# DeltaNet recurrence: both slots of filler of a chunk behind the new values' product, and the state's product with the queries behind the signal to VectorE

## The chip, the cores and the metric

The kernel runs on one core of one Trainium2 chip. A core has TensorE (matrix products, written PE in the profile, its weight loads PEld), VectorE (DVE), ScalarE (ACT), GpSimd (POOL) and SyncE (SP), which here issues most of the DMAs. Each engine works through a queue of its own in order; semaphores tie them together. The metric is the device time of one execution in microseconds (us), lower is better.

## The reference, cut to what matters

One layer of a hybrid decoder on 1024 positions of width 1024. Its second branch is a gated delta rule with four heads of dimension 128:

```
def step(state, inp):
    u_i, w_i, qd_i, qk_i, kt_i, gl_i = inp
    v_new = u_i - jnp.einsum('bhcd,bhde->bhce', w_i, state)
    o = jnp.einsum('bhcd,bhde->bhce', qd_i, state) + jnp.einsum('bhcj,bhje->bhce', qk_i, v_new)
    state = state * jnp.exp(gl_i)[..., None, None] + jnp.einsum('bhcd,bhce->bhde', kt_i, v_new)
    return state, o
```

It is a scan over chunks: each chunk's new values need the state, and the next state needs the new values. Around it stand a gMLP branch, stick-breaking attention, a wide input projection, a gated mix and a feed-forward network with 4096 hidden channels, all of them large products.

## The kernel before

The large products are made from blocks of 128 output channels. Each float32 operand is split into an upper and a lower part, so that one block is 2 halves of the positions x 8 slices of the depth = 16 steps, and one step is three 128x512 matmuls (`product_step`, lines 351 to 353). ScalarE makes the upper part of a block's weights (line 325), VectorE the lower (line 329), ScalarE evacuates each finished half (line 397, after steps 7 and 15 of the block).

In the phase that this change touches, the input projection's blocks of pairs 14 to 25 (384 steps) are executed beside the DeltaNet heads, as filler. Every engine walks the same list `DN_SLOTS` of weights: each call of `beside()` takes the next weight and executes as many steps as the rounded running sum allows. A weight of 1.2 is thus one step, now and then two. TensorE issues the matmuls of the steps, ScalarE and VectorE what belongs to them.

The heads i = 0 to 3 follow one another. A head first prepares its factors for all its chunks (two groups g of four chunks each, stages in `DN_STAGES`: Gram matrices, the triangular inverse by levels, the factor w), then scans its 8 chunks of 128 positions (n = 0 to 7). In the scan, chunk n on TensorE is:

- from chunk 1 on, a wait for the state (`dn_scan_ev`), then the state's product with the queries into the output bank (line 1369),
- the product of `d_TT` with `d_vb` (line 1370) and, from chunk 1 on, that of `d_wt` with the state (line 1372), which together are the new values; then a signal to VectorE,
- `beside()`, the first slot,
- a wait for VectorE's copy of the new values into `d_vn` (line 1782),
- the new values' share of the output (line 1376) and the state's product (line 1378), then a signal; VectorE makes the state `d_S` from it (line 1786 in chunk 0, line 1789 later),
- behind chunks 2 and 4 of heads 0 to 2 two sums of squares for the next head, and behind chunk 6 of each head one for the output's norm (line 1317),
- `beside()`, the second slot.

After chunk 7 follow a last slot of weight 4 and one more sum of squares. ScalarE uses the scan to activate the next head's inputs (lines 950 and 953), to load the function table and activate `d_z` (line 1008) and to make inverse roots (lines 959 and 962). VectorE has a piece of the next head's work behind each state (1699, 1703 and 1704, 1709, 1720, 1724), and both slots of a chunk behind that.

Of the kernel before, what the change touches and what calls it, by code (L numbers as in the profile page):

```python
# [13 lines left out]
NCH = S // P  # L14
# [44 lines left out]
def hybrid_decoder_layer(nc, xT, w_stream, w_bd, w_spT, cols_in, consts_in, outT):  # L59
# [12 lines left out]
    def sb(name, shape, dt=f32):  # L72
        return scope[0].enter_context(nc.sbuf_tensor(name, shape, dt))
# [4 lines left out]
    with top:  # L78
# [48 lines left out]
        with scope[0]:  # L127
            d_x = [sb(f"d_x{s}", [P, S]) for s in range(2)]
            d_z = sb("d_z", [P, S])
            d_q = sb("d_q", [P, S])  # L130
# [15 lines left out]
            d_S = sb("d_S", [P, P])  # L146
# [339 lines left out]
        def pe_beside(pe, b):  # L486
            for step in b.steps():
                blk, r = divmod(step, 16)
                hf, k = divmod(r, 8)
                n, s = b.n0 + blk // 2, blk % 2  # L490
                if k == 0:
                    pe.wait_ge(bank_read[hf], 1 + 2 * n + s)
                product_step(pe, n, s, hf, k, act_hi, act_lo)
# [50 lines left out]
        NDS = len(DN_STAGES)  # L544
# [3 lines left out]
        DN_FUNCS = (ACT.Identity, ACT.Gelu, ACT.Identity) * 4  # L548

        DN_PRO = [12, 3, 8]  # L550
        DN_HEAD = [2, 3, 1, 2, 1, 2, 1, 5] + [0, 2.72] * (NDS - 5) + [0, 1.5] + [1.2] * (2 * NCH) + [4]
        DN_SLOTS = DN_PRO + DN_HEAD * 4

        def dn_use(i, x):

            return 2 + DN_USES * i + x + 1

        def o_use(i):

            return dn_use(i, NDS + 2 if i < 3 else NDS)  # L560
# [606 lines left out]
        def _(pe):  # L1167
# [10 lines left out]
            for hf in range(2):  # L1178
                pe.wait_ge(bank_read[hf], 1)
                t = slice(HALF * hf, HALF * hf + HALF)  # L1180
                for k in range(KT):
                    for s in range(2):
# [7 lines left out]
                        o = first_banks[s][hf][:]  # L1190
# [33 lines left out]
            for n in range(NCH):  # L1224
                for part in range(2):
                    last = nc.tensor.matmul(c_bank[:, 8 * n:8 * n + 8], bdT[:, P * n:P * n + P], ident[0:16, 8 * part:8 * part + 8],
                                            start=(part == 0), stop=(part == 1))
# [80 lines left out]
            def beside():  # L1308
                pe_beside(pe, b)

            def chunk(t, n):
                return t[:, P * n:P * n + P]

            def squares_sum(g, sq, use):

                pe.wait_ge(dn_taken[g], use)
                nc.tensor.matmul(d_bank[g][:], ones[:], sq[:, HALF * g:HALF * g + HALF], start=True, stop=True).then_inc(dn_prod[g], 1)
# [8 lines left out]
            for i in range(4):  # L1326
                for x, name in enumerate(DN_STAGES):
                    for g in range(2):
                        pe.wait_ge(dn_taken[g], dn_use(i, x))
                        if name == "gram":  # L1330
                            pe.wait_ge(dn_ks, i + 1)
                        if name == "qk":
                            pe.wait_ge(dn_qs, i + 1)
                        if name == "vT":
                            pe.wait_ge(dn_silu, 3 * i + 3)
                        if name == "t0":
                            pe.wait_ge(dn_tt[g], i + 1)
                        if name[0] == "x":
                            pe.wait_ge(dn_b[g], (N_LEV - 1) * i + int(name[1:]))
                        for m in range(4):  # L1340
                            n = 4 * g + m
                            o = d_bank[g][:, P * m:P * m + P]
                            if name == "gram":
                                last = nc.tensor.matmul(o, chunk(d_x[1], n), chunk(d_x[1], n), start=True, stop=True)
                            elif name == "qk":
                                last = nc.tensor.matmul(o, chunk(d_x[1], n), chunk(d_q, n), start=True, stop=True)
                            elif name == "kT":
                                last = nc.tensor.transpose(o, chunk(d_x[1], n), ident)
                            elif name == "vT":
                                last = nc.tensor.transpose(o, chunk(d_x[2], n), ident)  # L1350
                            elif name[0] == "t":
                                last = nc.tensor.transpose(o, d_TT[:, n, :], ident)  # L1352
                            elif name[0] == "x":
                                last = nc.tensor.matmul(o, d_B[:, n, :], d_T[:, n, :], start=True, stop=True)  # L1354
                            elif name[0] == "y":
                                last = nc.tensor.matmul(o, d_X[:, n, :], d_TT[:, n, :], start=True, stop=True)  # L1356
                            else:
                                last = nc.tensor.matmul(o, d_kb[:, n, :], d_TT[:, n, :], start=True, stop=True)
                        last.then_inc(dn_prod[g], 1)
                        beside()  # L1360
                for n in range(NCH):
                    o = (z_bank[1] if n < 4 else c_bank)[:, P * (n % 4):P * (n % 4) + P]
                    if n == 1:
                        pe.wait_ge(dn_q, 2 * i + 2)
                        for g in range(2):
                            pe.wait_ge(dn_taken[g], 1 + dn_use(i, NDS - 1))
                    if n:
                        pe.wait_ge(dn_scan_ev, 15 * i + 2 * n)
                        nc.tensor.matmul(o, d_S[:], chunk(d_q, n), start=True, stop=False)
                    last = nc.tensor.matmul(z_bank[0][:, 0:P], d_TT[:, n, :], d_vb[:, n, :], start=True, stop=(n == 0))  # L1370
                    if n:
                        last = nc.tensor.matmul(z_bank[0][:, 0:P], d_wt[:, n, :], d_S[:], start=False, stop=True)
                    last.then_inc(dn_scan_mm, 1)
                    beside()
                    pe.wait_ge(dn_scan_ev, 15 * i + 2 * n + 1)
                    last = nc.tensor.matmul(o, d_vn[:], d_qk[:, n, :], start=(n == 0), stop=True)
                    if n < NCH - 1:
                        last = nc.tensor.matmul(z_bank[0][:, P:2 * P], d_kt[:, n, :], d_vn[:], start=True, stop=True)
                    last.then_inc(dn_scan_mm, 1)
                    if n in (2, 4) and i < 3:  # L1380
                        j = n // 2 - 1
                        pe.wait_ge(dn_sq, 2 * i + 2 + j + 1)
                        for g in range(2):
                            squares_sum(g, d_r[j], dn_use(i, NDS + j))
                    if n == 6:
                        pe.wait_ge(dn_osq, 2 * i + 1)
                        squares_sum(0, d_kb[:].rearrange("p n c -> p (n c)"), o_use(i))
                    beside()
                beside()
                pe.wait_ge(dn_osq, 2 * i + 2)  # L1390
                squares_sum(1, d_kb[:].rearrange("p n c -> p (n c)"), o_use(i))
# [17 lines left out]
            for b in range(4):  # L1409
# [3 lines left out]
                for hf in range(2):  # L1413
                    for m in range(4):
                        n = 4 * hf + m
# [14 lines left out]
            for i in range(2):  # L1430
                for q in range(6):
                    n, s = PAIR_BR + 3 * i + q // 2, q % 2
# [713 lines left out]
```

## Time and profile before

| | us |
|---|---|
| median of 3 runs | 1964.14 |
| lowest and highest | 1963.74, 1964.51 |
| the profiled execution | 1964.16 |
| its span in the profile | 1962.4 |

The span is the time between the first and the last instruction in the profile; the 1.8 us around it are start and end of the program. The four scans lie at about 559 to 588, 671 to 701, 782 to 811 and 891 to 917 us of the span. In the profile a product of 128x128 float32 shows as two matmuls (x2), a row names the first one's start, and a matmul's end is modelled, so distances between starts are to be read, not durations.

### The profile page before, as it was taken

The page shows a single profiled execution, that of the slowest core. Times are in us where ns is not written, and L with a number is a line of the kernel's source. Part 1 is how long each engine was busy: PE and PEld are TensorE (multiplying, and loading weights), DVE is VectorE, ACT ScalarE, POOL GpSimd, SP SyncE. Part 2 cuts the span into 40 slices and gives each one's busy share as a digit, 9 for nine tenths or more (in the row PEclk, how much of TensorE's full clock was granted, in tenths as well). Part 3 has the DMA queues.
Part 4 walks back from the last instruction along what each step waited for, and adds up shares of the span by engine and source line. Part 5 has one row for each costly group of instructions (what it writes and reads, how often), then busy time and mean ns, then how long its engine had stood idle before and what let it go on. Part 6 is the DMA issues. An engine that isn't in the chain of part 4 may idle for free.

```text
span 1962.4 us, 25291 instructions
## 1 busy us (share of the span) xinstructions
PE 1936.0 (99%) x9862; PEld 1576.8 (80%) x9862; DVE 945.3 (48%) x1267; ACT 759.5 (39%) x1165; POOL 83.2 (4%) x63
## 2 busy tenths in 40 slices
PE   9999999999999999999999999999999999999996
PEld 7887777777888888888787888888888888888885
DVE  6715566575445354523546654774333223223347
ACT  6325555554353543533334334543232113102322
POOL 0000000001203121120000000000000000000000
PEclk9999999999999999999999999999999999999998
DMA  5223122213122221223434444432311111111144
GB/s 193 98 97 118 51 92 97 103 49 140 65 97 86 97 87 65 86 74 129 153 133 152 134 147 149 150 130 92 107 45 52 53 43 46 50 53 43 49 155 150
DMA packets 62352, 191.75 MB, mean 98 GB/s; under 512 B 6768, under 2 KB 6832, under 8 KB 62256
## 3 DMA queue, kind: packets, MB, share of 16 engines
q1 hardware_dynamic: 59952, 186.23, 27.3%
q10 hardware_dynamic: 2304, 4.20, 0.6%
q8 instruction: 65, 1.06, 0.2%
q14 instruction: 31, 0.25, 0.0%
HBM read 146.33 MB, written 44.07 MB: 97 GB/s over the span
## 4 chain that ended last, share of the span: by engine, by line
PE 94%; DVE 3%; ACT 1%; issue 1%; DMA 1%; DVEq 0%; ACTq 0%; SPq 0%
PE gemm L351 18%; PE gemm L353 18%; PE gemm L352 18%; PE gemm L595 6%; PE gemm L597 5%; PE gemm L596 5%; PE dn L1354 2%; PE dn L1356 2%; PE z L1253 2%; PE gemm L1442 2%; PE dn L1275 2%; PE gemm L1443 2%; PE gemm L1444 2%; PE dn L1352 1%; PE attn_out L1287 1%; PE cumsum L1287 1%
## 5 line engine op out<-in xcount | busy, mean ns | idle before, releaser
L351 PE MATMUL gemm<-act_hi,w_hi 128*128 128x512 f32 x1216 | 500.9, 412 | 0.5 <-issue 0.5
L353 PE MATMUL gemm<-act_hi,w_lo 128*128 128x512 f32 x1216 | 476.1, 392 | 0.0
L352 PE MATMUL gemm<-act_lo,w_hi 128*128 128x512 f32 x1216 | 474.8, 390 | 0.0
L329 DVE TENSOR_TENSOR w_lo<-w_raw,w_hi 128x1024 fp32r<-128x1024 f32 x174 | 217.3, 1249 | 194.0 <-ACT w_hi L325 190.5
L325 ACT ACTIVATE w_hi<-w_raw 128x1024 fp32r<-128x1024 f32 x174 | 183.1, 1052 | 280.8 <-PE gemm L353 153.2
L353 PEld LDWEIGHTS gemm<-act_hi,w_lo 128*128 128x128 f32 x1216 | 228.6, 188 | 49.6
L351 PEld LDWEIGHTS gemm<-act_hi,w_hi 128*128 128x128 f32 x1216 | 229.5, 189 | 45.8 <-issue 6.7
L352 PEld LDWEIGHTS gemm<-act_lo,w_hi 128*128 128x128 f32 x1216 | 229.7, 189 | 43.0 <-issue 3.3
L397 ACT ACTIVATE stage<-gemm,cols 128x512 f32<-128x512 f32 x104 | 71.6, 688 | 239.7 <-PE gemm L353 235.6
L1117 ACT ACTIVATE f_t<-f_t 128x512 f32<-128x512 f32 x64 | 40.4, 632 | 218.0 <-DVE f_t L1959 218.0
L1629 DVE TENSOR_TENSOR_SCAN a_P<-a_keep,a_P,a_floor 128x512 f32<-128x512 f32 (+3 forms) x96 | 94.0, 1008 | 37.6 <-ACT a_keep L912 37.2
L595 PE MATMUL gemm<-act_hi,w_hi 128*128 128x512 f32 x256 | 101.3, 396 | 0.9 <-DVE w_lo L329 0.7
L2065 POOL TENSOR_TENSOR d_bB<-d_at,consts 128x512 f32<-128x512 f32 x48 | 66.5, 1404 | 793.3 <-DVE d_at L1761 630.5
L595 PE MATMUL gemm<-f_hi,w_hi 128*128 128x512 f32 x256 | 100.0, 391 | 0.0
L597 PE MATMUL gemm<-act_hi,w_lo 128*128 128x512 f32 x256 | 99.7, 390 | 0.0
L596 PE MATMUL gemm<-act_lo,w_hi 128*128 128x512 f32 x256 | 99.7, 389 | 0.0
L597 PE MATMUL gemm<-f_hi,w_lo 128*128 128x512 f32 x256 | 99.6, 389 | 0.0
L596 PE MATMUL gemm<-f_lo,w_hi 128*128 128x512 f32 x256 | 99.6, 389 | 0.0
L351 PE MATMUL gemm<-f_hi,w_hi 128*128 128x512 f32 x256 | 99.6, 389 | 0.0
L352 PE MATMUL gemm<-f_lo,w_hi 128*128 128x512 f32 x256 | 99.6, 389 | 0.0
L353 PE MATMUL gemm<-f_hi,w_lo 128*128 128x512 f32 x256 | 99.6, 389 | 0.0
L1775 DVE TENSOR_TENSOR d_TT<-d_TT,dn 128x512 f32<-128x512 f32 x48 | 33.0, 688 | 134.7 <-PE dn L1356 134.7
(280 smaller groups left out, 2888.1 us busy)
## 6 DMA issues: line engine op xcount, KB each, us to landing
w_raw<-w_stream SPq DMA_DIRECT2D x174, 512.0 KB, 3.4
projections<-stage SPq DMA_DIRECT2D x60, 512.0 KB, 2.9
gate<-projections SPq DMA_DIRECT2D x48, 256.0 KB, 2.7
d_in<-projections SPq DMA_DIRECT2D x12, 512.0 KB, 6.8
x_fin<-xT SPq DMA_DIRECT2D x8, 512.0 KB, 4.3
residual<-mixed ACTq DMA_DIRECT2D x16, 256.0 KB, 2.0
act_hi<-residual SPq DMA_DIRECT2D x8, 512.0 KB, 4.9
outT<-mixed SPq DMA_DIRECT2D x16, 256.0 KB, 2.0
```

The source lines that it names most:

```text
L325: nc.scalar.activation(w_hi[s][:], w_raw[s][:].rearrange("p (k c) -> p k c", k=KT), ACT.Copy).then_inc(hi_ready[s], 1)
L329: nc.vector.tensor_tensor(w_lo[s][:], w_raw[s][:].rearrange("p (k c) -> p k c", k=KT), w_hi[s][:].bitcast(f32), ALU.subtract).then_inc(lo_ ...
L351: nc.tensor.matmul(g_bank[hf][:], w_hi[s][:, k, :], a_hi[:, k, t], start=(k == 0), stop=False)
L352: nc.tensor.matmul(g_bank[hf][:], w_hi[s][:, k, :], a_lo[:, k, t], start=False, stop=False)
L353: last = nc.tensor.matmul(g_bank[hf][:], w_lo[s][:, k, :], a_hi[:, k, t], start=False, stop=(k == KT - 1))
L397: nc.scalar.activation(stage[s][:, HALF * hf:HALF * hf + HALF], g_bank[hf][:], func, bias=cols[:, ds(V_BIN + 2 * (n + shift) + s, 1)]).the ...
L595: nc.tensor.matmul(g_bank[s][:], w_hi[s][:, k, :], a_hi[:, k, t], start=(k == 0), stop=False)
L596: nc.tensor.matmul(g_bank[s][:], w_hi[s][:, k, :], a_lo[:, k, t], start=False, stop=False)
L597: last = nc.tensor.matmul(g_bank[s][:], w_lo[s][:, k, :], a_hi[:, k, t], start=False, stop=(k == KT - 1))
L1117: nc.scalar.activation(f_t[slot][:], f_t[slot][:], ACT.Square).then_inc(f_sqr, 1)
L1629: nc.vector.tensor_tensor_scan(run[:, off:off + n][:, ::-1], a_keep[Y % 4][:, 0:n][:, ::-1], floor[:, ::-1], run[:, off + n:off + n + 1], ...
L2065: nc.gpsimd.tensor_tensor(d_B[:, c, :], d_at[:, c, :], consts[:, None, C_LEV + lev, :].broadcast_to([P, 4, P]), ALU.mult).then_inc(dn_b[g], 1)
```

## The change

In the scan the two slots of a chunk had a weight of 1.2 each. Now the first has 2.4 and the second 0.0; the sum is the same, so that all steps outside the scan stay in their slots. And the state's product with the queries no longer stands ahead of the new values' products, but behind their signal and ahead of the first slot. The wait for the state stays where it was, ahead of the chunk's first product.

```diff
-        DN_HEAD = [2, 3, 1, 2, 1, 2, 1, 5] + [0, 2.72] * (NDS - 5) + [0, 1.5] + [1.2] * (2 * NCH) + [4]
+        DN_HEAD = [2, 3, 1, 2, 1, 2, 1, 5] + [0, 2.72] * (NDS - 5) + [0, 1.5] + [2.4, 0.0] * NCH + [4]
...
                     if n:
                         pe.wait_ge(dn_scan_ev, 15 * i + 2 * n)
-                        nc.tensor.matmul(o, d_S[:], chunk(d_q, n), start=True, stop=False)
                     last = nc.tensor.matmul(z_bank[0][:, 0:P], d_TT[:, n, :], d_vb[:, n, :], start=True, stop=(n == 0))
                     if n:
                         last = nc.tensor.matmul(z_bank[0][:, 0:P], d_wt[:, n, :], d_S[:], start=False, stop=True)
                     last.then_inc(dn_scan_mm, 1)
+                    if n:
+                        nc.tensor.matmul(o, d_S[:], chunk(d_q, n), start=True, stop=False)
                     beside()
```

The orders below give the lines of each kernel's own code: behind the moved product, 1370, 1372, 1369, 1376 and 1378 of before are 1369, 1371, 1374, 1377 and 1379 of after. TensorE, head 0, from chunk 1's share of the output to chunk 2's first slot, before:

```order
L1376 MATMUL z<-d_qk,d_vn 128x128 [waits dn_scan_ev]
L1378 MATMUL z<-d_vn,d_kt 128x128
L351 MATMUL gemm<-act_hi,w_hi 128x512
L352 MATMUL gemm<-act_lo,w_hi 128x512
L353 MATMUL gemm<-act_hi,w_lo 128x512
L1369 MATMUL z<-d_q,d_S 128x128 [waits dn_scan_ev]
L1370 MATMUL z<-d_vb,d_TT 128x128
L1372 MATMUL z<-d_S,d_wt 128x128
L351 MATMUL gemm<-act_hi,w_hi 128x512
L352 MATMUL gemm<-act_lo,w_hi 128x512
L353 MATMUL gemm<-act_hi,w_lo 128x512
```

The same place after:

```order
L1377 MATMUL z<-d_qk,d_vn 128x128 [waits dn_scan_ev]
L1379 MATMUL z<-d_vn,d_kt 128x128
L1369 MATMUL z<-d_vb,d_TT 128x128 [waits dn_scan_ev]
L1371 MATMUL z<-d_S,d_wt 128x128
L1374 MATMUL z<-d_q,d_S 128x128
L351 MATMUL gemm<-act_hi,w_hi 128x512
L352 MATMUL gemm<-act_lo,w_hi 128x512
L353 MATMUL gemm<-act_hi,w_lo 128x512
L351 MATMUL gemm<-act_hi,w_hi 128x512
L352 MATMUL gemm<-act_lo,w_hi 128x512
L353 MATMUL gemm<-act_hi,w_lo 128x512
```

The step (351 to 353) between the state's product on `d_kt` and the wait for `dn_scan_ev` is gone from there and has become one more step in the first slot; the product of `d_q` with `d_S` now follows the other two.

ScalarE, head 2, around its chunk 0, before (`stage` is the evacuation of a finished half, `w_hi` the upper part of the next weights, `d_z`, `d_x` and `d_r` belong to the head itself):

```order
L1008 ACT_TABLE_LOAD
L1008 ACTIVATE d_z<-d_z 128x1024 [waits dn_z]
L950 ACTIVATE d_x<-d_x 128x1024 [waits dn_conv]
L953 ACTIVATE d_r<-d_x 128x1024 [waits dn_silu]
L397 ACTIVATE stage<-gemm,cols 128x512 [waits blk_done0]
L325 ACTIVATE w_hi<-w_raw 128x1024 [waits blk_done0,raw_loaded0]
L950 ACTIVATE d_x<-d_x 128x1024 [waits dn_conv]
```

After:

```order
L397 ACTIVATE stage<-gemm,cols 128x512 [waits blk_done0]
L325 ACTIVATE w_hi<-w_raw 128x1024 [waits blk_done0,raw_loaded0]
L1008 ACT_TABLE_LOAD
L1008 ACTIVATE d_z<-d_z 128x1024 [waits dn_z]
L950 ACTIVATE d_x<-d_x 128x1024 [waits dn_conv]
L953 ACTIVATE d_r<-d_x 128x1024 [waits dn_silu]
L950 ACTIVATE d_x<-d_x 128x1024 [waits dn_conv]
```

The evacuation and the weight split of the step that moved to the first slot now stand ahead of the table load and of the head's own activations. There are six such moves on ScalarE in the four scans; VectorE's and SyncE's orders are the same in both kernels.

## Rows read from the trace of the kernel before

**Rows 1.** The page's head: the span, then busy time of each engine.
```profile
span 1962.4 us, 25291 instructions
...
PE 1936.0 (99%) x9862; PEld 1576.8 (80%) x9862; DVE 945.3 (48%) x1267; ACT 759.5 (39%) x1165; POOL 83.2 (4%) x63
```

**Rows 2.** Waits of TensorE's weight loads, 550 to 930: us, times, longest.
```profile
PEld z L1376 <- DVE d_vn L1782: 1.8, 3, 1.3
```

**Rows 3.** Timeline, head 3, chunks 4 to 6: start us, duration us, engine, line.
```profile
902.43 0.39 PE L1372 MATMUL z<-d_S,d_wt 128*128 128x128 f32 x2
...
903.58 0.39 PE L1378 MATMUL z<-d_vn,d_kt 128*128 128x128 f32 x2
...
904.00 0.35 DVE L1789 SCALAR_TENSOR_TENSOR d_S<-d_S,d_last,z 128x128 f32<-128x128 f32 x1 [0.85 <-PE z L1378]
...
904.40 0.30 PEld L1369 LDWEIGHTS cumsum<-d_q,d_S 128*128 128x128 f32 x2 [0.18 <-DVE d_S L1789]
904.50 0.40 PE L1369 MATMUL cumsum<-d_q,d_S 128*128 128x128 f32 x2
...
904.96 0.39 PE L1372 MATMUL z<-d_S,d_wt 128*128 128x128 f32 x2
...
906.77 0.39 PE L1378 MATMUL z<-d_vn,d_kt 128*128 128x128 f32 x2
```

**Rows 4.** Timeline, head 1, chunk 1: VectorE's queue held by a DMA.
```profile
673.34 0.39 PE L1372 MATMUL z<-d_S,d_wt 128*128 128x128 f32 x2
...
673.72 1.23 DVE L1699 TENSOR_TENSOR d_dt<-d_gB,bd_gc 128x1024 f32<-128x1024 f32 x1 [1.05 <-DMA d_bB<-decay_beta_rows]
...
675.65 0.39 PE L1378 MATMUL z<-d_vn,d_kt 128*128 128x128 f32 x2
```

**Rows 5.** Timeline, head 0: the copy behind chunk 0, then chunk 1's products.
```profile
560.54 0.29 DVE L1786 COPY d_S<-z 128x128 f32<-128x128 f32 x1 [0.86 <-PE z L1378]
...
561.50 0.39 PE L1372 MATMUL z<-d_S,d_wt 128*128 128x128 f32 x2
...
562.78 0.39 PE L1378 MATMUL z<-d_vn,d_kt 128*128 128x128 f32 x2
```

**Rows 6.** Timeline of TensorE: sums of squares behind chunks 2 and 6.
```profile
566.23 1.88 PE L1317 MATMUL dn<-d_r,ones 128*128 128x512 f32 x4
...
568.64 0.38 PE L1369 MATMUL z<-d_q,d_S 128*128 128x128 f32 x2
...
909.51 1.02 PE L1317 MATMUL dn<-d_kb,ones 128*128 128x512 f32 x2
...
911.07 0.38 PE L1369 MATMUL cumsum<-d_q,d_S 128*128 128x128 f32 x2
```

**Rows 7.** Timeline of VectorE, head 1, behind chunk 6.
```profile
693.44 0.35 DVE L1789 SCALAR_TENSOR_TENSOR d_S<-d_S,d_last,z 128x128 f32<-128x128 f32 x1 [0.83 <-PE z L1378]
693.71 1.22 DVE L1720 TENSOR_TENSOR d_dt<-d_dt,consts 128x1024 f32<-128x1024 f32 x1
694.96 1.23 DVE L329 TENSOR_TENSOR w_lo<-w_raw,w_hi 128x1024 fp32r<-128x1024 f32 x1
```

**Rows 8.** Timeline, head 2, chunk 0: TensorE's first product, then ScalarE.
```profile
781.76 0.38 PE L1370 MATMUL z<-d_vb,d_TT 128*128 128x128 f32 x2
...
781.87 1.28 ACT L1008 ACT_TABLE_LOAD   x1
...
786.17 0.67 ACT L397 ACTIVATE stage<-gemm,cols 128x512 f32<-128x512 f32 x1
...
787.69 1.05 ACT L950 ACTIVATE d_x<-d_x 128x1024 f32<-128x1024 f32 x1
```

**Rows 9.** Timeline, start of head 1: a weight load behind a bank's wait.
```profile
589.55 0.97 PEld L1344 LDWEIGHTS dn<-d_x 128*128 128x128 f32 x8 [1.67 <-ACT d_wt L959]
```

**Rows 10.** Stretches: engines' busy us, granted clock (the number after POOL), DMA.
```profile
130.80:137.60 6.80, 6.80 (x24) 5.90 (x25) 1.53 (x4) 4.53 (x7) 0.00 (x0) 0.50 0.97 360
...
671.00:696.00 25.00, 24.10 (x132) 18.73 (x132) 9.64 (x20) 17.99 (x22) 0.00 (x0) 1.00 0.45 162
```

## The prediction, made before the changed kernel had run

> **What bounds the kernel now.** I read four views in this order. The page's head gives the size of the question: TensorE is busy 1936.0 of 1962.4 us, so whatever makes it stand still in the recurrence is added to the end, and what makes another engine faster is not taken off it [rows 1]. The waits of TensorE's weight loads over the whole stretch of the four heads tell how much there is to gain: its longest entry from the chunks is 1.8 us in 3 waits for the new values [rows 2]. So both hand-overs to VectorE in a chunk are covered today, each by one step of filler (three 128x512 matmuls). The timeline of one chunk shows by how much, and that is the row set on which the forecast rests [rows 3]. The timelines of chunks with a wait, of the chunks that have other products between state and next chunk, and of ScalarE's queue give the exceptions [rows 4 to 8]. I call the heads 0 to 3 and the chunks 0 to 7, "new values" the copy on line 1782, "state" the update on line 1789 (a copy on 1786 in chunk 0).
>
> **Units, from [rows 3].** Two 128x128 products lie between 904.50 and 904.96, so one takes 0.23 us. From a chunk's last product before the filler to its state product is 1.15 us with one step (902.43 to 903.58) and 1.81 us with two (904.96 to 906.77): a step costs 0.67 us when it joins another. The state product starts at 903.58 and has left TensorE at 903.80; VectorE starts the state at 904.00 and needs 0.35; the load of the product that waits for it stands at 904.40 and the product at 904.50. From 903.80 to 904.50 are 0.70 us, and the one filler step there covers them (0.67 us and 0.03 of hand-over).
>
> **Part 1, the filler step behind the state product goes away.** The change leaves the wait for the state in front of the chunk's first product (the order shows it there, now on the product of d_TT with d_vb, though this one reads no state). The distance of 0.70 us is made of VectorE's answer and the load, neither of which the filler shortened, so TensorE stands still for it. It applies where nothing else lies between: not behind chunks 2 and 4 of heads 0 to 2, where two sums of squares take 568.64 - 566.23 - 0.67 = 1.74 us, and not behind chunk 6 of any head, where one takes 911.07 - 909.51 - 0.67 = 0.89 us [rows 6]; both are longer than 0.70. Seven boundaries by four heads are 28; less 6 and less 4 leave 18. Four of them follow chunk 0, whose copy takes 0.29 instead of 0.35 us [rows 5]: 0.64 each. 14 x 0.70 + 4 x 0.64 = **+12.4 us**. Bounds: if the answer came as fast as a product's own end allows in [rows 3] less the 0.10 between load and product, 0.60 each, +10.6; if each wait cost 0.10 more, +14.2.
>
> **Part 2, the same step stands behind the new values' product.** The steps are the same 19 or 20 a head and each is still executed; in its new place it costs 0.67 us instead of 0.70, since it shares the hand-over: 28 x 0.03 = **-0.8 us** (between 0 and -0.8).
>
> **Part 3, the new values get more cover.** In a chunk with one step in that place, TensorE now has 0.67 us more filler and 0.23 us of the state's product with the queries, which moves behind the signal. Moving it costs nothing by itself, it is one product either way. It removes the waits that exist. In head 1 the row differences wait for a DMA and hold VectorE's queue (line 1699 at 673.72), so that chunk 1 takes 675.65 - 673.34 = 2.31 us instead of 1.15: 1.16 us [rows 4]. The DMA's time doesn't move, TensorE comes 1.3 us later by then (one step and one wait) and has two further steps: all of it goes. In head 0 the same place has 562.78 - 561.50 = 1.28, 0.13 too much [rows 5]. Together **-1.3 us** (0 to -2).
>
> **Part 4, one place where cover gets thinner.** Everything that VectorE does between the state and the next new values (up to 1.2 us for a split, scaling or mask) used to hide under two steps and three products; now it hides under one chunk's first slot. With two steps there TensorE needs the new values 0.15 + 3 x 0.23 + 1.37 = 2.2 us after the state's end (904.35 in [rows 3]); with one 1.25 us instruction between, VectorE has them ready for a product after 1.25 + 0.29 + 0.15 = 1.7. It holds. In head 1 behind chunk 6 there are two (the mask at 693.71, the weight split at 694.96) [rows 7]. VectorE would finish the new values 0.47 + 1.25 + 1.23 + 0.29 = 3.24 us after the square sum starts, the dependent product comes 0.15 later: 3.39. TensorE is there after 0.89 + 3 x 0.23 + 2 x 0.67 + 0.03 = 2.95. **+0.45 us** (0 to 1). VectorE's and SyncE's own orders don't change; no load or store is issued in another place.
>
> **Part 5, ScalarE.** Six evacuations move ahead of the head's own activations. The hardest is head 2, chunk 0: the evacuation and the weight split now stand ahead of the table load. The head's first product starts at 781.76. Today ScalarE runs on at once, from the table load at 781.87 to the end of the square at 786.17, and then 1.5 us of evacuation and split until 787.69 [rows 8]. Then it would wait for the head's second step, which ends at 781.76 + 0.23 + 0.03 + 1.34 = 783.4, be done with both at 785.1, and with the square 4.3 us later, at 789.4. TensorE needs that square behind chunk 2. Chunk 0 takes it 0.23 + 2.04 + 0.46 (three steps), the wait 0.64; chunks 1 and 2 take 0.69 + 1.37 + 0.46 each (two steps), the wait between them 0.70: 781.76 + 9.11 = 790.9. **0**, with 1.5 us to spare; if that cover were gone, up to 1.6 us, the time ScalarE now stands in front of the step, and the same once more in head 1.
>
> **Sum.** 12.4 - 0.8 - 1.3 + 0.45 = +10.8 us. Against the profiled execution, 1964.16 us with a span of 1962.4, it gives 1975.0; that execution is within 0.1 us of the median of 1964.14, so the sum holds for both.
>
> **A rule weighed.** In every case of this trace where TensorE waits on a semaphore, the weight load waits too: the load of line 1344 needs only keys that have long been there, the wait is for a PSUM bank, and the load still stands idle 1.67 us until ScalarE has emptied it [rows 9]. The Trainium skill, "TensorE: Matmul & The Clock Gate", section "Architectural detail: the array is 16x 32x32, not 1x 128x128", states that TensorE's queue is a partial reorder window and can pull weight loads ahead of matmuls in flight. By that rule the load of d_TT, which needs no state, would slip in front of the wait. The trace's row speaks against it here.
>
> **Rivals.**
> (a) The load goes ahead of the wait. The distance from load to product in [rows 3], 904.40 to 904.50, is saved 18 times, 1.8 us: 1973.2. Against it: [rows 9].
> (b) ScalarE falls behind by the bounds of part 5, 2 x 1.6 us: 1978.2. For it: it waits for filler before the activations that the sums of squares need. Against: TensorE itself is slower by then, and there is 1.5 us to spare.
> (c) The clock falls. In head 1's chunks the granted clock is 1.00, that is 2.4 GHz; one stretch of 6.80 us in the trace has 0.50, that is 1.2 GHz [rows 10]. Such a stretch costs half its length, 3.4 us; one in each head gives 1975.0 + 13.6 = 1988.6. For it: TensorE stands still for a fifth of a chunk. Against: the wait of 1.16 us in head 1 lies in that stretch and left the clock at 1.00.
> (d) Not slower. The state's wait is cheaper than I read: TensorE still has matmuls in flight when the wait begins, and if the answer cost nothing beyond them, the parts 2 to 4 would be left, -1.65 us: 1962.5. It decides at a price of 1.65 / 18 = 0.09 us a boundary. Against: VectorE starts 0.20 us after the product has left and needs 0.35, two terms that nothing on TensorE can hide.
> That the change doesn't do what it says is excluded by the order: the filler rows between the two products are gone.
>
> **How the numbers follow.** Forecast 0.74, (a) 0.08, (b) 0.12, (c) 0.03, (d) 0.03. The forecast's own bounds: the 0.60 to 0.80 of part 1 is -1.8 to +1.8, the parts 2 to 4 add -0.9 to +1.9, not all at once; I take 1972.2 to 1978.4, which holds (a) and most of (b) and leaves out (c), (d) and the ends. A measurement of this kernel tells 0.2% (3.9 us) from no change; only (d) lies within it. Slower 0.96, same 0.03, faster 0.01.
>
> **What would show it.** In the profile after, TensorE's weight load of the product of d_TT with d_vb waits for the state in about 18 places, 0.5 to 0.7 us each, about 11 us in all; the waits for new values shrink to one in head 1, chunk 7; the chunk with two steps takes 3.2 us instead of 2.5; the square sums have no wait on ScalarE in front; the granted clock stays 1.00. It would be wrong if these waits were short, or if the heads' stretches grew by something other than them.

## The result, and the profile after

| | before | after |
|---|---|---|
| median | 1963.89 us (5 runs, 1962.45 to 1964.51) | 1973.81 us (5 runs, 1973.40 to 1975.41) |
| profiled execution, span | 1962.4 us | 1971.6 us |

The changed kernel takes 1.0053 times as long (95% interval 1.0039 to 1.0068): 9.9 us more, where 10.8 were forecast. The head of the page after, to be held against [rows 1]: the engines' busy times differ by 3.2 us at most (TensorE's matmuls 1938.6 against 1936.0), the span is 9.2 us longer.

```profile
span 1971.6 us, 25291 instructions
...
PE 1938.6 (98%) x9862; PEld 1580.0 (80%) x9862; DVE 944.3 (48%) x1267; ACT 759.4 (39%) x1165; POOL 83.1 (4%) x63
```

The waits of TensorE's matmuls over the four heads (engine, what waited, for whom: us in total, times, longest). Both entries are new; a matmul's end is modelled, so they show the number of the stills better than their length:

```profile
PE z L1369 <- DVE d_S L1790: 6.2, 14, 0.4
PE z L1369 <- DVE d_S L1787: 1.9, 4, 0.5
```

The product of `d_TT` with `d_vb` waits 14 times for the state's update and 4 times, behind chunk 0, for its copy: 18 stills. The same view of the weight loads, as in [rows 2], needs care:

```profile
PEld z L1369 <- DVE d_S L1790: 10.5, 18, 0.6
PEld z L1369 <- issue: 5.4, 16, 0.6
...
PEld cumsum L1377 <- DVE d_vn L1783: 0.5, 1, 0.5
```

Its 18 waits for the state are not the 18 stills. They are 14 of 0.63 us and 4 of 0.41 behind chunk 6, where the sum of squares still runs and no matmul waits; the four stills behind chunk 0, of 0.64 us each on the load, stand under "issue". The waits for new values of [rows 2] are down to one of 0.5 us.

One chunk and the next in head 3, to be held against [rows 3] (start us, duration us, engine, line):

```profile
905.58 0.38 PE L1377 MATMUL z<-d_qk,d_vn 128*128 128x128 f32 x2
...
905.80 0.39 PE L1379 MATMUL z<-d_vn,d_kt 128*128 128x128 f32 x2
...
906.23 0.35 DVE L1790 SCALAR_TENSOR_TENSOR d_S<-d_S,d_last,z 128x128 f32<-128x128 f32 x1 [2.44 <-PE z L1379]
...
906.63 0.30 PEld L1369 LDWEIGHTS z<-d_vb,d_TT 128*128 128x128 f32 x2 [0.63 <-DVE d_S L1790]
...
906.95 0.39 PE L1371 MATMUL z<-d_S,d_wt 128*128 128x128 f32 x2
...
908.79 0.38 PE L1377 MATMUL z<-d_qk,d_vn 128*128 128x128 f32 x2
```

The order is now 1377, 1379, then nothing, then 1369 and 1371. From the state product's start to the start of the product of `d_wt` with the state are 906.95 - 905.80 = 1.15 us; two products, the state's and 1369, take 0.45 of it, so 0.70 us stand still. VectorE's answer is what it was: it starts 0.43 after the product's start (0.42 in [rows 3]) and the load starts 0.05 after its end. The load does not read the state and waits all the same.

How long the scans take is read from TensorE's timeline, from the start of a head's first product of `d_TT` with `d_vb` to that of its last sum of squares. For head 3, before:

```profile
891.00 0.38 PE L1370 MATMUL z<-d_vb,d_TT 128*128 128x128 f32 x2
...
916.80 1.02 PE L1317 MATMUL dn<-d_kb,ones 128*128 128x512 f32 x2
```

and after, 29.96 instead of 25.80 us:

```profile
896.17 0.38 PE L1369 MATMUL z<-d_vb,d_TT 128*128 128x128 f32 x2
...
926.13 1.02 PE L1317 MATMUL dn<-d_kb,ones 128*128 128x512 f32 x2
```

| head | 0 | 1 | 2 | 3 | sum |
|---|---|---|---|---|---|
| before, us | 28.72 | 29.68 | 28.54 | 25.80 | 112.74 |
| after, us | 31.28 | 31.65 | 31.25 | 29.96 | 124.14 |
| difference | 2.56 | 1.97 | 2.71 | 4.16 | 11.40 |

The scans alone lose 11.4 us. The rest of the span is 1849.7 us before and 1847.5 after, 2.2 less, in code that the change doesn't touch; what the profiles show of it is in the last section.

### The profile page after: what moved, and what is told of

It reads as the page before. It is cut to its first block, busy times and chain, and to the rows that moved or that the text cites. A ratio compares the mean times of both kernels' runs of the same rounds, so it can differ in the third digit from the quotient of the medians.

```text
span 1971.6 us, 25291 instructions
## 1 busy us (share of the span) xinstructions
PE 1938.6 (98%) x9862; PEld 1580.0 (80%) x9862; DVE 944.3 (48%) x1267; ACT 759.4 (39%) x1165; POOL 83.1 (4%) x63
## 4 chain that ended last, share of the span: by engine, by line
PE 94%; DVE 3%; ACT 1%; issue 1%; DMA 0%; DVEq 0%; ACTq 0%; SPq 0%
PE gemm L351 18%; PE gemm L353 18%; PE gemm L352 18%; PE gemm L595 6%; PE gemm L596 5%; PE gemm L597 5%; PE dn L1354 2%; PE dn L1356 2%; PE z L1253 2%; PE gemm L1443 2%; PE dn L1275 2%; PE gemm L1445 2%; PE gemm L1444 2%; PE dn L1352 1%; PE attn_out L1287 1%; PE cumsum L1287 1%
```

## The experiments

All of them are read twice: by the median against runs of the kernel before on the same chip, and by the sum of the four scans in the profiled execution. The second is the sharper one: the same TensorE and VectorE order gave 124.14 and 124.15 us in two kernels (after and e4). The groups of experiments ran on different chips, and a difference of medians between two of them, say e6 less after, is rougher than one to the kernel before.

| kernel | slots | sum of scans, us | less before | median, us | ratio, 95% interval |
|---|---|---|---|---|---|
| before | 1.2, 1.2 | 112.74 | | 1963.3 to 1963.9 | |
| after | 2.4, 0.0 | 124.14 | +11.40 | 1973.81 | 1.0053 (1.0039 to 1.0068) |
| e1, slots alone | 2.4, 0.0 | 124.19 | +11.45 | 1973.21 | 1.0052 (1.0035 to 1.0069) |
| e2, product alone | 1.2, 1.2 | 113.07 | +0.33 | 1962.47 | 0.9996 (0.9986 to 1.0006) |
| e3, slots mirrored | 0.0, 2.4 | 126.34 | +13.60 | 1976.84 | 1.0070 (1.0054 to 1.0087) |
| e4, ScalarE's old order | 2.4, 0.0 | 124.15 | +11.41 | 1974.62 | 1.0061 (1.0044 to 1.0078) |
| e5, head 3 alone | mixed | 116.96 | +4.22 | 1966.97 | 1.0019 (1.0010 to 1.0028) |
| e6, free product ahead | 2.4, 0.0 | 120.24 | +7.50 | 1970.00 | 1.0035 (1.0021 to 1.0048) |
| e7, and state product first | 2.4, 0.0 | 116.01 | +3.27 | 1965.80 | 1.0015 (1.0005 to 1.0024) |
| e8, both reorderings | 1.2, 1.2 | 112.87 | +0.13 | 1962.65 | 0.9997 (0.9988 to 1.0006) |
| e9, and rows later | 1.2, 1.2 | 111.25 | -1.49 | 1961.09 | 0.9987 (0.9978 to 0.9996) |
| e10, and tiny products mixed | 1.2, 1.2 | 111.20 | -1.54 | 1960.48 | 0.9989 (0.9980 to 0.9998) |
| e11, mixed finer | 1.2, 1.2 | 111.19 | -1.55 | 1962.26 | 0.9994 (0.9985 to 1.0003) |

**Each half of the change alone.** The slots without the moved product:

```diff
-        ... + [0, 1.5] + [1.2] * (2 * NCH) + [4]
+        ... + [0, 1.5] + [2.4, 0.0] * NCH + [4]
```

> One part alone: the slots are 2.4 and 0.0 as in the changed kernel, the state's product with the queries stays ahead of the new values' products. Theory (TensorE stands still 0.70 us for the state at 18 boundaries, since the filler behind the state product is gone): +12.4 for the stills, -0.8 for shared hand-overs, -1.3 for the waits for new values that go, +0.7 in head 1 chunk 7, where the product no longer gives 0.23 us of cover: +11.0 us on before, and 18 waits for the state of about 0.6 us each on the weight loads. Rival (the moved product is what costs): no more than +1 us.

Measured: +11.45 us in the scans, the same as the whole change. The waits of TensorE's matmuls, where the product with the queries (1369 here, as in the kernel before) meets the state's wait:

```profile
PE cumsum L1369 <- DVE d_S L1789: 4.0, 9, 0.4
PE z L1369 <- DVE d_S L1789: 2.2, 5, 0.4
PE z L1369 <- DVE d_S L1786: 1.9, 4, 0.5
```

Nine, five and four are the 18 places. The slots are the whole loss, and the moved product has no part in it.

The moved product alone is the changed kernel with `[1.2] * (2 * NCH)` put back.

> The other part alone: the state's product with the queries moves behind the signal, the slots stay 1.2 and 1.2. Theory: it costs nothing by itself and gives each wait for new values 0.23 us of cover; the wait in head 1 chunk 1 falls from 1.16 to 0.93 us, the 0.13 in head 0 goes: -0.4 us on before, not to be told from no change, no wait for the state over 0.2 us. Rival (the moved product costs): +5 us or more.

Measured: +0.33 us in the scans, 0.9996 in time. The rival is out: the move costs nothing. But one step of the expectation was wrong: the wait in head 1 didn't shrink by 0.23 us, nor did the 0.13 us in head 0 go. In the timeline of head 1:

```profile
670.96 0.38 PE L1369 MATMUL z<-d_vb,d_TT 128*128 128x128 f32 x2
...
674.11 1.23 DVE L1700 TENSOR_TENSOR d_dt<-d_gB,bd_gc 128x1024 f32<-128x1024 f32 x1 [1.29 <-DMA d_bB<-decay_beta_rows]
...
675.72 0.30 PEld L1377 LDWEIGHTS z<-d_qk,d_vn 128*128 128x128 f32 x2 [1.59 <-DVE d_vn L1783]
```

VectorE gets its rows at 674.11, 3.15 us after the head's first product (2.90 before, [rows 4] less the head's start at 670.82), and the load's wait is 1.59 instead of 1.33 us long. In head 0 VectorE's differences wait 0.18 us for the DMA of their rows, where they didn't wait before, and the state product comes 0.30 us later than in a chunk without a wait (0.13 before). The product with the queries stood ahead of the wait for new values before and still does; only its place among the work ahead of it changed. A wait whose end is set by a DMA didn't get cheaper by that. In the changed kernel, where a step comes in from behind the wait, it is gone.

**The mirror image.** `[0.0, 2.4] * NCH` in place of `[2.4, 0.0] * NCH`, all filler behind the state product.

> The mirror image: slots 0.0 and 2.4, so that all filler of a chunk stands behind the state product, the moved product as in the changed kernel. Theory (each hand-over to VectorE costs its full distance when nothing covers it): from the end of a new values' product to the product that waits for them 0.64 us, less 0.23 for the moved product in chunks 1 to 7: 4 x 0.64 + 28 x 0.41 = 14.0, less 0.4 in head 1 where a DMA sets the moment, less 0.9 for shared hand-overs, +0.6 in head 1 chunk 7: +13.3 us on before; the 18 waits for the state are gone. Rival (only the state's hand-over is dear, the loss has to do with the state): +3 us or less.

Measured: +13.60 us in the scans, +13.4 in time. All 32 chunks now wait for new values, and no load waits for the state:

```profile
PEld z L1377 <- DVE d_vn L1783: 7.2, 16, 0.9
PEld cumsum L1377 <- DVE d_vn L1783: 5.7, 16, 0.4
```

So the price lies on whichever hand-over stands bare. This one is cheaper a place, because the moved product covers a part of it: 1.09 us from the product of `d_wt` to the state product, less three products of 0.23, leave about 0.4 in chunks 1 to 7. It is the dearer in sum, because it comes 32 times, without the sums of squares that cover 10 of the 28 others.

**ScalarE.** TensorE and VectorE as changed, ScalarE with the old list:

```diff
+        ACT_HEAD = DN_HEAD[:-2 * NCH - 1] + [1.2] * (2 * NCH) + [4]
+        ACT_SLOTS = DN_PRO + ACT_HEAD * 4
...
-            b = Beside(PAIR_DN, DN_SLOTS, DN_FUNCS)
+            b = Beside(PAIR_DN, ACT_SLOTS, DN_FUNCS)
```

> TensorE and VectorE as in the changed kernel, ScalarE keeps the order of the kernel before (its evacuations stand where the slots 1.2 and 1.2 put them). Theory: ScalarE's order has no part in it, the time is that of the changed kernel within 0.5 us. Rival (ScalarE's six moved evacuations cost a part): 1 to 3 us less than the changed kernel.

Measured: 124.15 us in the scans against 124.14, with the same waits to the digit (the edit shifts lines by two):

```profile
PE z L1371 <- DVE d_S L1792: 6.2, 14, 0.4
PE z L1371 <- DVE d_S L1789: 1.9, 4, 0.5
```

Rival (b) is out.

**A third of the dose.** The list of head 3 alone gets the new slots.

```diff
+        DN_SLOTS = DN_PRO + DN_HEAD * 3 + DN_HEAD[:-2 * NCH - 1] + [2.4, 0.0] * NCH + [4]
```

> The slots 2.4 and 0.0 in head 3 alone, 1.2 and 1.2 in the others, the product moved in all. Theory (a fixed price for each uncovered boundary): head 3 has six of the 18, 0.64 + 5 x 0.70 - 7 x 0.03 = +3.9 us, its stretch from the first product to the last sum of squares is 29.9 instead of 25.8 us; the other heads as with the product alone. +3.9 us on before, about a third of the changed kernel's loss. Rival (a loss that comes from the three heads with ScalarE work, or that grows with the heads): under 1 or over 6 us.

Measured: head 3 takes 29.92 us (29.96 in the changed kernel), the others 28.67, 29.84 and 28.53, as in e2; 1.0019 in time, 3.7 us. Six of the 18 places, a little over a third of the loss (4.22 of 11.40 us). The price is the same a place as in the whole change, and no ScalarE work of a next head takes part in head 3.

**Filling the still from inside.** The changed kernel, with the product that reads no state ahead of the wait. The state product gets the bank `attn_out`, which is unused in this phase, so that TensorE doesn't write the bank that VectorE is reading, and VectorE takes it from there. The product and the bank were not changed one at a time.

```diff
+                    last = nc.tensor.matmul(z_bank[0][:, 0:P], d_TT[:, n, :], d_vb[:, n, :], start=True, stop=(n == 0))
                     if n == 1:
...
                     if n:
                         pe.wait_ge(dn_scan_ev, 15 * i + 2 * n)
-                    last = nc.tensor.matmul(z_bank[0][:, 0:P], d_TT[:, n, :], d_vb[:, n, :], start=True, stop=(n == 0))
...
-                        last = nc.tensor.matmul(z_bank[0][:, P:2 * P], d_kt[:, n, :], d_vn[:], start=True, stop=True)
+                        last = nc.tensor.matmul(o_bank[:, 0:P], d_kt[:, n, :], d_vn[:], start=True, stop=True)
```

> The changed kernel with one thing in the still: the product of d_TT with d_vb, which reads no state, goes ahead of the wait for the state; so that VectorE's reading stays on a bank of its own, the state product is written to the unused bank attn_out. Theory: each still shrinks by that product, 18 x 0.23 = 4.1 us less than the changed kernel, about 1969.7 us. Rival (a still is a fixed time after the load that waits, or TensorE's queue already loads ahead): no more than 1 us less.

Measured: 3.9 us less than the changed kernel in the scans, 3.8 in time. Head 3, chunk 1 to 2:

```profile
898.28 0.39 PE L1379 MATMUL attn_out<-d_vn,d_kt 128*128 128x128 f32 x2
...
898.50 0.39 PE L1363 MATMUL z<-d_vb,d_TT 128*128 128x128 f32 x2
898.70 0.35 DVE L1790 SCALAR_TENSOR_TENSOR d_S<-d_S,d_last,attn_out 128x128 f32<-128x128 f32 x1 [1.77 <-PE attn_out L1379]
899.10 0.30 PEld L1371 LDWEIGHTS z<-d_S,d_wt 128*128 128x128 f32 x2 [0.41 <-DVE d_S L1790]
```

VectorE starts 0.42 after the state product as ever (898.70 - 898.28), but TensorE is at work on 1363 meanwhile, and the load stands idle 0.41 instead of 0.63 us. It bears on rival (a): what the queue did by itself in none of the 18 stills of the changed kernel is worth 0.22 us a place (3.9 / 18) when the program does it, product and load together. The Trainium skill ("TensorE: Matmul & The Clock Gate", section "Architectural detail: the array is 16x 32x32, not 1x 128x128") has weight loads pulled ahead of matmuls in flight; in those 18 stills the load, which reads no state, was not pulled ahead of the semaphore's wait; it stood idle 0.63 or 0.64 us.

Then the state product goes ahead of the output's as well (the count that ScalarE waits for in chunk 3 is raised by one to match):

```diff
+                    if n < NCH - 1:
+                        nc.tensor.matmul(o_bank[:, 0:P], d_kt[:, n, :], d_vn[:], start=True, stop=True).then_inc(dn_scan_mm, 1)
                     last = nc.tensor.matmul(o, d_vn[:], d_qk[:, n, :], start=(n == 0), stop=True)
-                    if n < NCH - 1:
-                        last = nc.tensor.matmul(o_bank[:, 0:P], d_kt[:, n, :], d_vn[:], start=True, stop=True)
-                    last.then_inc(dn_scan_mm, 1)
+                    if n == NCH - 1:
+                        last.then_inc(dn_scan_mm, 1)
```

> As the run before, and the state product goes ahead of the output's product on d_vn, so that VectorE gets its signal one product earlier. Theory: each still shrinks to 0.70 - 2 x 0.23 = 0.24 us (0.18 behind chunk 0), 8.3 us less than the changed kernel, about 1965.5 us, still some 2 us more than before. Rival: as before.

Measured: 8.1 us less than the changed kernel in the scans, 8.0 in time, 3.3 and 2.5 more than before.

```profile
894.09 0.38 PE L1378 MATMUL attn_out<-d_vn,d_kt 128*128 128x128 f32 x2
...
894.31 0.39 PE L1379 MATMUL z<-d_qk,d_vn 128*128 128x128 f32 x2
...
894.51 0.35 DVE L1791 SCALAR_TENSOR_TENSOR d_S<-d_S,d_last,attn_out 128x128 f32<-128x128 f32 x1 [1.54 <-PE attn_out L1378]
894.53 0.39 PE L1363 MATMUL z<-d_vb,d_TT 128*128 128x128 f32 x2
894.91 0.30 PEld L1371 LDWEIGHTS z<-d_S,d_wt 128*128 128x128 f32 x2 [0.18 <-DVE d_S L1791]
```

Two products now run between the state product and the product that waits, and 894.91 - 894.53 - 0.23 = 0.15 us plus the load's 0.1 are left of the 0.70.

**Both reorderings with the old slots,** that is e7 with `[1.2] * (2 * NCH)`.

> Both reorderings of the run before, with the slots at 1.2 and 1.2 as in the kernel before. Theory: both hand-overs are covered with room, only the wait for new values in head 1 behind the DMA is left (about 1 us): -0.5 us on before (-1.5 to +0.3), which a few rounds can hardly tell. Rival (the reorderings themselves cost or give something beyond the cover): over 2 us either way.

Measured: +0.13 us in the scans, 0.9997 in time. Nothing is bare, so there is nothing for them to fill; head 1 keeps its wait for the DMA (29.96 us), as in e2.

**The rows one chunk later,** on top of e8:

```diff
-                        if n == 0:
+                        if n == 1:
                             differences(i + 1)
-                        if n == 1:
+                        if n == 2:
                             limited(i + 1)
```

> As the kernel with the slots at 1.2 and 1.2 and both reorderings, and VectorE takes the next head's row differences behind chunk 1 instead of chunk 0 (the limiting behind chunk 2 instead of 1), so that the DMA of the rows has a chunk longer. Theory: the last wait for new values in head 1 goes (1.2 to 1.6 us in the profiles so far), -1.8 us on before and 1.2 less than that kernel. Rival (VectorE's work only moves its wait to the next chunk): no change.

Measured: head 1 takes 28.50 us, like heads 0 and 2 (28.52, 28.48); -1.49 in the scans, ratio 0.9987 with an interval that leaves out 1. VectorE's wait is gone, not moved: the state update is followed at once by the differences, and the next new values come when TensorE has them.

```profile
673.85 0.35 DVE L1791 SCALAR_TENSOR_TENSOR d_S<-d_S,d_last,attn_out 128x128 f32<-128x128 f32 x1 [0.85 <-PE attn_out L1378]
...
674.12 1.22 DVE L1701 TENSOR_TENSOR d_dt<-d_gB,bd_gc 128x1024 f32<-128x1024 f32 x1
...
675.98 0.29 DVE L1784 COPY d_vn<-z 128x128 f32<-128x128 f32 x1 [0.64 <-PE z L1371]
```

## Why the prediction was right

**The bound.** TensorE's order was the right place to look: the engines are as busy as before, and the time lost in the scans is the time of the new waits, less that of the old ones that went.

**The stills, part 1.** Eighteen were forecast and 18 are there. The price was 0.70 us; it is 0.70, in all of them. Only the discount of the four behind chunk 0 is missing: there too the next product comes 1.16 us after the state product's start. The copy is 0.06 us shorter, yet the load behind it stands idle 0.64 us, as long as behind the update. The trace of the kernel before has it already: in head 0 the copy of [rows 5] ends at 560.54 + 0.29 = 560.83, and the load starts 0.12 us later, not 0.05 as in [rows 3]:

```profile
560.95 0.30 PEld L1369 LDWEIGHTS z<-d_q,d_S 128*128 128x128 f32 x2 [0.19 <-issue]
```

It is the load that waits for four semaphores (`dn_q` and two of `dn_taken` beside the state's), and the profile puts its idle time down to issue. That this is the reason was not tested. It is +0.2 us.

**The shared hand-over, part 2,** is the term that was mis-sized. Head 3 has nothing but six stills, 4.2 us, and grew by 4.16: the saving is below 0.1 there and about 0.3 in all, not 0.8. A step that joins another costs 0.69 us and not 0.67: in e2 the distance from the product of `d_wt` to the state product is 1.36 us with one step and 2.05 with two, in the changed kernel 2.05 with two and 2.74 with three. The 0.67 came from one pair of chunks, 1.15 and 1.81; other chunks with two steps have 1.84. Nor was the 0.03 us a hand-over of the step: part of it was the start of the wait for the state itself, which [rows 3] show as 0.18 us of idle load. In e8, where no load waits for the state, the distance from the state product to the product of `d_wt` is 1.36 instead of 1.38 us.

**More cover, part 3.** The waits for new values of 1.16 and 0.13 us went as said. e2 and e8 show that it was the step moved in front that did it, not the moved product, which I had counted along with it.

**Less cover, part 4.** Head 1, chunk 7, after, to be held against [rows 7]:

```profile
696.96 1.02 PE L1317 MATMUL dn<-d_kb,ones 128*128 128x512 f32 x2
...
697.43 1.22 DVE L1721 TENSOR_TENSOR d_dt<-d_dt,consts 128x1024 f32<-128x1024 f32 x1
...
698.27 0.39 PE L1374 MATMUL cumsum<-d_q,d_S 128*128 128x128 f32 x2
...
698.68 1.23 DVE L329 TENSOR_TENSOR w_lo<-w_raw,w_hi 128x1024 fp32r<-128x1024 f32 x1
...
699.83 0.28 DVE L1783 COPY d_vn<-z 128x128 f32<-128x128 f32 x1
...
700.16 0.30 PEld L1377 LDWEIGHTS cumsum<-d_qk,d_vn 128*128 128x128 f32 x2 [0.55 <-DVE d_vn L1783]
```

The state and the two long instructions stand between 696.96 and VectorE's copy at 699.83, and TensorE, with its second step over at 698.27 + 0.23 + 1.37 = 699.87, gets to its product only at 700.16 + 0.11. That is 0.40 us, forecast were 0.45. It is the one 0.5 in the waits after.

**ScalarE, part 5.** It stands 1.80 us in front of the step in head 2, then runs through; the square that TensorE needs starts at 791.09, is over at 792.15, and TensorE takes it at 793.36 (line 1317). 1.2 us to spare, where 1.5 were forecast:

```profile
786.11 0.69 ACT L397 ACTIVATE stage<-gemm,cols 128x512 f32<-128x512 f32 x1 [1.80 <-PE gemm L353]
...
791.09 1.06 ACT L953 ACTIVATE d_r<-d_x 128x1024 f32<-128x1024 f32 x1
...
793.36 1.88 PE L1317 MATMUL dn<-d_r,ones 128*128 128x512 f32 x4
```

**The sum** by what was measured is 18 x 0.70 = 12.6, and 12.6 - 0.3 - 1.3 + 0.4 = 11.4, which are the 11.4 in the scans. The forecast of 10.8 was low by 0.6, and the median came out at 9.9 because of something outside the scans, below, of which the forecast said nothing. The bounds of the parts 2 to 4 were added up too narrowly: by their own figures they are -1.15 and +2.65 us around the forecast, not -0.9 and +1.9. The measured time lies within either.

**The rivals.** (a), the load ahead of the wait: no, the loads of all 18 stills wait for 0.63 or 0.64 us. (b), ScalarE: no, by e4. (c), the clock: the granted clock is 1.00 in all four scans of the changed kernel, the upper level of 2.4 GHz, with a fifth of a chunk idle. (d), a cheap wait: no, 0.70 us a place where it needed 0.09. What remains argued and not shown is why VectorE starts 0.20 us after a product has left TensorE; no run changes that distance.

## What to carry to other kernels

Where two hand-overs alternate on the bounding engine, filler pays only up to the length of the hand-over it covers: 0.7 us here. A second piece behind the same one bought nothing where no wait was left to cover, and its missing twin cost the whole distance each time, so the count of bare places times that distance was nearly the whole forecast. Before adding filler, look in the program for products that don't need what the wait is for: they fill it from inside (0.22 us each here, with the state product in a PSUM bank of its own; without that bank it wasn't run). And the wait that ended with a DMA went when its consumer moved a chunk later (e9), or when work from behind it came in front (the change); another order of the work in front of it didn't help (e2).

## What was not expected

The scans lost 11.4 us and the median 9.9. Over all profiled executions the rest of the span, which no edit up to e9 touches, falls into three groups: 1849.1 to 1849.7 us (before, e2, e3, e9), 1846.8 to 1848.4 (after, e4, e5, e6, e8) and 1846.1 to 1846.6 (e1, e7). The difference lies at one place, in and behind a row of 32 tiny matmuls of 16x8 (line 1226), which takes 3.73 us after and in e7. Before, where the clock falls while it runs, it takes 5.02:

```profile
128.62 5.02 PE L1226 MATMUL cumsum<-consts,bdT 16*128 16x8 f32 x32
133.57 0.80 PE L351 MATMUL gemm<-act_hi,w_hi 128*128 128x512 f32 x1
134.17 0.63 PE L352 MATMUL gemm<-act_lo,w_hi 128*128 128x512 f32 x1
```

The first two 128x512 matmuls behind them last 0.80 and 0.63 us; in e7 they last 0.50 and 0.40. In the stretch from 131.00 to 137.80 us the granted clock, the number after POOL's, is 0.51 before (1.2 GHz nearly all the way),

```profile
131.00:137.80 6.80, 6.80 (x23) 5.90 (x23) 1.33 (x4) 4.53 (x7) 0.00 (x0) 0.51 0.95 349
```

0.75 after (half of it at 1.2 GHz),

```profile
131.00:137.80 6.80, 6.80 (x29) 5.64 (x29) 1.29 (x5) 5.73 (x11) 0.00 (x0) 0.75 0.96 341
```

and 1.00 in e7, with 36 matmuls in the same time instead of 23:

```profile
131.00:137.80 6.80, 6.80 (x36) 5.82 (x36) 1.29 (x5) 5.64 (x11) 0.00 (x0) 1.00 0.93 339
```

At 1.2 GHz a stretch costs half its length, an estimate of 3.4 us for all of this one; the rest of the span differs by 3.6 between before and e7. Each of the eleven executions profiled up to e9 has about the whole of it, half or nothing. It goes along with the runs' times too: the 77 runs of the kernel before beside the experiments average 1964.2 us at a mean granted clock of 0.995 (35 runs), 1962.8 at 0.996 (35) and 1961.9 at 0.997 (7). Within one of these groups they still differ by 1.5 to 3.0 us, which this doesn't explain. Compared group by group the change costs 11.0, 10.6 and 11.9 us (two, two and one run after), nearer to the 11.4 of the scans than the 9.9 of the medians; with so few runs that is an indication.

Two kernels test it, both on top of e9:

```diff
-            for n in range(NCH):
-                for part in range(2):
...
-            pe_block(pe, N_SB - 1, 0, act_hi, act_lo, 0)
+            for k in range(KT):
+                product_step(pe, N_SB - 1, 0, 0, k, act_hi, act_lo)
+                for n in range(2 * k, min(NCH, 2 * k + 2)):
+                    for part in range(2):
...
+            product_half(pe, N_SB - 1, 0, 1, act_hi, act_lo, 2 * (N_SB - 1))
```

> As the kernel with the slots at 1.2 and 1.2, both reorderings and the rows one chunk later; and the 32 tiny matmuls of 16x8 at 128 us of the span (line 1226), which stand in one row, are put two channels' worth behind each of the next four steps of the projection. In the profiles so far the granted clock fell to 0.50 right behind that row for 6.8 us (before and three others), for about half of that (five) or not at all (two), and the rest of the program outside the scans was 3.4, 1.7 or 0 us longer, in the same order. Theory (the row of tiny matmuls is what the clock falls behind): mixed with large ones it doesn't fall, the granted clock is 1.00 from 128 to 142 us, 1 to 3.4 us less than the kernel without the mixing, about 1959 us, and less scatter. Rival (the fall comes from something else of that moment, such as the DMAs there): the clock falls as often.

Measured: in the profile the clock stays up, and the tiny products stand in four groups of eight.

```profile
128.99 1.05 PE L1229 MATMUL cumsum<-consts,bdT 16*128 16x8 f32 x8
129.97 0.50 PE L351 MATMUL gemm<-act_hi,w_hi 128*128 128x512 f32 x1
...
130.87 1.05 PE L1229 MATMUL cumsum<-consts,bdT 16*128 16x8 f32 x8
```

```profile
131.00:134.40 3.40, 3.40 (x22) 2.76 (x22) 0.39 (x1) 0.44 (x1) 0.00 (x0) 1.00 1.01 329
```

But of 11 runs seven came at 1959.9 to 1960.6 us with a mean clock of 0.997, two at 1962.2 and 1962.9 (0.996) and two at 1964.6 and 1965.2 (0.995). By their mean clocks it still falls in some; no profile shows where, and the two slowest are over 4 us behind the seven, more than the 3.4 us above. The median of 1960.48 is the lowest of all kernels here, 0.9989 of before (0.9980 to 0.9998), and not to be told from e9's.

With one pair of products behind each of eight steps instead:

> As the run before with one channel's worth behind each of the next eight steps. Theory: as there, the clock stays at 1.00; the products come 2.7 us later, which the vectors behind them have room for. Rival: as there, or a longer mixed stretch at which the clock falls later.

Measured: 11 runs lie between 1961.94 and 1962.59 us, all with a mean clock of 0.997 or 0.998; no other kernel here had so narrow a spread with so many runs. In the profile the clock is 1.00 while the DMAs (the last number but one) are as busy as ever:

```profile
131.00:134.40 3.40, 3.40 (x20) 2.53 (x19) 0.92 (x1) 0.96 (x1) 0.00 (x0) 1.00 1.00 345
```

So the unbroken row of tiny matmuls is what the clock falls in or behind, and the DMAs of that moment alone are not. But the finer mixing costs about as much as the fall: 1962.26 is 1.8 us more than e10 on the same chip, and the rest of the span is 1849.3 us, as in the kernels with the whole fall, against 1847.0 in e10. A part of that is on TensorE: its groups of four start 1.43 us apart with a step between them and those of e10, of eight, 1.87. Less 0.69 a step that is 8 x 0.74 = 5.9 us against 4 x 1.18 = 4.7, and 3.73 for the single row, so splitting it costs TensorE time by itself. Where the remaining 1.1 us between e11 and e10 come from wasn't found; the products also come later for the vectors that need them.
